# Narrow sample tables, merge ahead of residual, and a queries-and-keys stage that opens on tiles still on chip

## The reference

```python
mod = (silu(c) @ w_ada + b_ada)                       # sh1, sc1, g1, sh2, sc2, g2
h = rms_norm(x, norm1_g) * (1 + sc1) + sh1
q, k, v, u = split(h @ w_in)                          # 512, 512, 512, 1024 columns
q, k = rms_norm of each head (8 heads x 64)
new_k, new_v = the last 2048 positions of keys and values
# attention: three dilated windows (w, d) = (128, 1), (512, 4), (2048, 16): keys at distance
# 0 <= dist <= w with dist % d == 0, relative bias by log bucket, and the three outputs merged:
w = exp(m_p - max_p m_p);  o = sum(w * acc_p) / sum(w * l_p)
glu = u[:512] * sigmoid(u[512:])
dw = causal depthwise conv of glu over 31 positions (30 rows of history for the sample)
o_conv = silu(layer_norm(dw)) @ w_pw2
x = x + g1 * (concat(o_attn, o_conv) @ w_o)
h2 = rms_norm(x, norm2_g) * (1 + sc2) + sh2
x = x + g2 * (square(relu(h2 @ w_ff1)) @ w_ff2)
```

## Time and profile before

| | us |
|---|---|
| median of three runs | 3102.84 (3100.72 to 3103.69) |
| profiled execution, its own time | 3098.28 |
| its span in the profile | 3096.5 |
| TensorE busy | 2817.3 (91%) |
| VectorE, ScalarE, GpSimd busy | 1349.0, 910.5, 636.4 |
| mean granted TensorE clock | 0.951 |
| stages start at | 0, 85.0, 448.5, 689.2, 1097.7, 1241.6, 1592.3 |

### The profile page before, as it was taken

How to read it: one execution, slowest core, us unless ns; L and a number is a source line. 1 busy time by engine, 2 the same in 40 slices (tenths; PEclk the granted TensorE clock), 3 DMA queues, 4 the chain that set the end, 5 groups by cost and what they waited for, 6 DMA issues and landing times. The chain is left out here.

```text
span 3096.5 us, 40055 instructions
## 1 busy us (share of the span) xinstructions
PE 2817.3 (91%) x15078; PEld 2329.9 (75%) x15078; DVE 1349.0 (44%) x3393; ACT 910.5 (29%) x2077; POOL 636.4 (21%) x420
## 2 busy tenths in 40 slices
PE   5899979969999955788869999999997999999998
PEld 2677748847777732467648888888887999999998
DVE  3148879976777532466642111122232222222223
ACT  2333311115565521344431222211131211222211
POOL 0000000000000000244423333333332323333331
PEclk6899989979999978899989999999999999999999
DMA  7566536636553374344441213131243311111112
GB/s 245 186 205 234 196 129 225 219 102 194 174 195 116 110 272 191 104 162 139 156 148 60 91 47 101 48 102 48 85 122 133 99 48 48 48 42 48 48 48 106
DMA packets 289237, 392.95 MB, mean 127 GB/s; under 512 B 30042, under 2 KB 238282, under 8 KB 282634
## 3 DMA queue, kind: packets, MB, share of 16 engines
q1 hardware_dynamic: 266194, 298.27, 29.7%
q0 software_dynamic: 5376, 81.84, 7.4%
q10 hardware_dynamic: 17476, 10.28, 1.1%
HBM read 311.63 MB, written 150.84 MB: 149 GB/s over the span
## 5 line engine op out<-in xcount | busy, mean ns | idle before, releaser
L2337 PE MATMUL ff_u_ps<-ff_h_hi,ff_w_hi 128*128 128x352 f32 (+1 forms) x1280 | 452.1, 353 | 18.8 <-DVE ff_h_lo L2255 17.2
L2338 PE MATMUL ff_u_ps<-ff_h_lo,ff_w_hi 128*128 128x352 f32 (+1 forms) x1280 | 450.0, 352 | 0.0
L2339 PE MATMUL ff_u_ps<-ff_h_hi,ff_w_lo 128*128 128x352 f32 (+1 forms) x1280 | 449.4, 351 | 0.0
L2337 PE MATMUL ff_u_ps<-ff_a_hi,ff_w_hi 128*128 128x352 f32 (+1 forms) x1280 | 449.2, 351 | 0.0
L2338 PE MATMUL ff_u_ps<-ff_a_lo,ff_w_hi 128*128 128x352 f32 (+1 forms) x1280 | 448.7, 351 | 0.0
L2339 PE MATMUL ff_u_ps<-ff_a_hi,ff_w_lo 128*128 128x352 f32 (+1 forms) x1280 | 448.2, 350 | 0.0
L2185 POOL TENSOR_TENSOR ff_w_lo<-ff_w_raw,ff_w_hi 128x1024 fp32r<-128x1024 f32 x128 | 306.6, 2395 | 570.3 <-ACT ff_w_hi L2210 570.3
L2295 DVE TENSOR_TENSOR ff_sqr<-ff_relu 128x352 f32<-128x352 f32 (+1 forms) x160 | 98.7, 617 | 640.6 <-ACT ff_relu L2238 640.6
L2278 DVE SCALAR_TENSOR_TENSOR ff_y<-ff_u_ps,modT,ff_y 128x512 f32<-128x512 f32 (+2 forms) x280 | 178.8, 644 | 432.3 <-PE ff_u_ps L2339 432.3
L2210 ACT ACTIVATE ff_w_hi<-ff_w_raw 128x1024 fp32r<-128x1024 f32 x128 | 134.7, 1052 | 626.9 <-PE ff_u_ps L2339 605.3
L2337 PEld LDWEIGHTS ff_u_ps<-ff_h_hi,ff_w_hi 128*128 128x128 f32 x1280 | 241.6, 189 | 45.0 <-POOL ff_w_lo L2185 17.3
(11 more groups left out here) (269 smaller groups left out, 4375.3 us busy)
## 6 DMA issues: line engine op xcount, KB each, us to landing
ff_w_raw<-in_w_ff_dram SPq DMA_DIRECT2D x128, 512.0 KB, 3.8
out_new_k_sample_dram<-in_cache_k_dram POOLq DMA_DIRECT2D x8, 4088.0 KB, 15.4
out_new_v_sample_dram<-in_cache_v_dram POOLq DMA_DIRECT2D x8, 4088.0 KB, 15.9
dwq<-in_w_ada_dram SPq DMA_DIRECT2D x32, 512.0 KB, 7.9
gluT<-in_cache_k_dram SPq DMA_DIRECT2D x16, 1024.0 KB, 15.0
sa_vn<-in_cache_v_dram SPq DMA_DIRECT2D x16, 1024.0 KB, 16.5
mx_acc<-acc_d SPq DMA_DIRECT2D x16, 768.0 KB, 8.2
vu_x_in<-in_x_prompt_dram SPq DMA_DIRECT2D x16, 512.0 KB, 13.5
```

What stands on the lines that cost most here:

```text
L2337: pe.matmul(out, w_hi[:, b, w], hi, start=first, stop=False)
L2338: pe.matmul(out, w_hi[:, b, w], lo, start=False, stop=False)
L2339: return pe.matmul(out, w_lo[:, b, w], hi, start=False, stop=last)
```

## The change

The diff has these parts:

- **Tables.** A pattern's table has only the columns that it can use: 4 × 128 + 4 = 516 in place of 1028. In patterns 0 and 1 these are the last 512 cached keys and the new ones, in pattern 2 the new ones and the 512 strided keys. Seven pieces (3 for the prompt, 4 of 387 columns for the sample) in place of 12, all inside the loop over k.
- **rsqrt.** A Newton step has three instructions in place of four.
- **Values stage.** The early conv operations lie on tiles 4 to 15; `store_piece(1)` and the four weight loads are issued at tile 15; the last two tiles' `h_hi`, `h_lo` stay on chip (`last_hi`, `last_lo`) and are not stored.
- **Queries and keys.** The order of tiles is 16, 15, 0, 1, ... 14 (`tile_at`). The product of z with the norm moves from VectorE to ScalarE, 16 copies with a scale (`scaled`); the key gain moves behind the late conv operations, which lie on 15 tiles.
- **Sample attention.** Queries have a semaphore of their own (`q_in`), the cached keys 8 to 15 are loaded ahead of the second half's values, softmax and values of half 0 come ahead of the transposes of half 1 on all engines, no copy of the scores, the division by the sum is part of `gather`, one of the copies of the transposed probabilities is ScalarE's, and the store of the output is waited for only in the next stage.
- **Merge stage.** Its statistics, first two accumulators and first two conv tiles are loaded in sample attention; the fold's copies come ahead of most of the splits; GpSimd merges tile i + 2 ahead of the residual of tile i; behind the loads of tile 10 two weights and four pieces of h for the MLP are loaded.
- **MLP.** It begins with these.

```diff
-SKEYS = 4 * P + 4 * P + DS
+SKEYS = 4 * P + DS
...
             for _ in range(3):
-                step(v.tensor_tensor(t, y, y, ALU.mult))
+                step(v.scalar_tensor_tensor(out=t, in0=y, scalar=-0.5, in1=y, op0=ALU.mult, op1=ALU.mult))
                 step(v.tensor_tensor(t, t, a, ALU.mult))
-                step(v.tensor_scalar(t, t, -0.5, 1.5, ALU.mult, ALU.add))
-                step(v.tensor_tensor(y, y, t, ALU.mult))
+                step(v.scalar_tensor_tensor(out=y, in0=t, scalar=1.5, in1=y, op0=ALU.add, op1=ALU.mult))
...
-                        for g in range(KT, NTB):
-                            table(g)
+                            if k < NTB:
+                                table(k)
...
+                            if i >= NT - 1:
+                                return
...
+                                sp.wait_ge(q_pe, 2 * NQ)
+                                for k in range(4):
+                                    load_qk_w(sp, k)
+                                store_piece(1)
...
-                            mine = early_ops[5 * (i - 4):5 * (i - 3) if i < NT else 2 * TAPS] if i >= 4 else []
+                            mine = early_ops[2 * TAPS * (i - 4) // 12:2 * TAPS * (i - 3) // 12] if 4 <= i < NT else []
...
+                tile_at = [NT, NT - 1] + list(range(NT - 1))
...
                         load_h(2)
-                        for i in range(NT + 1):
-                            if i + HB <= NT:
-                                load_h(i + HB)
-                            if i >= 1:
-                                store_k(i - 1)
-                            if i >= 3:
-                                store_t(i - 3)
+                        for k in range(4, KT):
+                            sp.wait_ge(w_lod, k - 3)
+                            load_qk_w(sp, k)
+                        for half in range(2):
+                            sp.dma_start(qgain[half * DH:(half + 1) * DH, :], I["q_norm_g"][0].rearrange("(d o) -> d o", o=1)).then_inc(gain_in, 16)
+                        sp.dma_start(kgain[:], I["k_norm_g"].to_broadcast([P, DH])).then_inc(gain_in, 16)
+                        for u in range(NT + 1):
+                            if u + HB <= NT:
+                                load_h(u + HB)
+                            if u >= 1:
+                                store_k(u - 1)
+                            if u >= 3:
+                                store_t(u - 3)
...
+                        def scaled(u):
+                            n = rows_of(tile_at[u])
+                            act.wait_ge(rs_done, u + 1)
+                            if u >= 2:
+                                act.wait_ge(t_pe, 2 * (u - 1))
+                                act.wait_ge(k_out[u % 2], k_stored(u - 2))
+                            for h in range(2 * H):
+                                z = z_ps[(2 * u + h // H) % 6][0:n, h % H * DH:(h % H + 1) * DH]
+                                ins = act.activation(nrm[0:n, u % 2, h * DH:(h + 1) * DH], z, ACT.Copy, scale=rsq[0:n, u % 2, h:h + 1])
+                            ins.then_inc(z_free, 1)
...
+                        squares(0)
+                        for u in range(NT + 1):
+                            scaled(u)
+                            if u + 1 <= NT:
+                                squares(u + 1)
+                            if u >= 1:
+                                turned(u - 1)
...
+                            head_norms(u)
+                            for o in range(QK_OPS * u // (NT - 1), QK_OPS * min(u + 1, NT - 1) // (NT - 1)):
                                 late_op(v, cstep, o)
+                            key_gain(u)
...
+                    sp.dma_start(vnew[:], O["new_v_sample"][0, :, WINC - DS:WINC].rearrange("b t h d -> t b (h d)")).then_inc(b_in, 16)
+                    for j in range(G):
+                        load_v(0, j, 1)
+                    for n in range(2 * G, 4 * G):
+                        load_k(n)
+                    sp.wait_ge(o_pe, 1)
                     for a in range(2):
-                        sp.dma_start(vn[:, 0, a], cache_rows(I["cache_v"], 0, a)).then_inc(v_in, 16)
-                    sp.dma_start(vnew[:], O["new_v_sample"][0, :, WINC - DS:WINC].rearrange("b t h d -> t b (h d)")).then_inc(small_in, 16)
-                    sp.dma_start(sbias[:].rearrange("p a c -> p (a c)"), sbias_d).then_inc(small_in, 16)
-                    for g in range(DB // G):
-                        for b in range(G * g, G * g + G):
-                            if b % G == 0 and g >= 1:
-                                sp.wait_ge(o_pe, g)
-                            for a in range(2):
-                                if b >= 1:
-                                    sp.dma_start(vn[:, b % G, a], cache_rows(I["cache_v"], b, a)).then_inc(v_in, 16)
-                            for n in (range(2 * b + 4, 2 * b + 6 + (b == G - 1)) if b < G else range(2 * b + 5, 2 * b + 7)):
-                                if n < 2 * DB:
-                                    load_k(n)
-                    sp.wait_ge(k_pe, 8 * DB)
-                    sp.dma_start(wp_raw, I["w_pw2"][0].rearrange("(k p) c -> p k c", p=P)).then_inc(wp_in, 16)
-                    sp.dma_start(wl_raw, I["w_o"][0, AW:D, :].rearrange("(k p) c -> p k c", p=P)).then_inc(wl_in, 16)
-                    for g in range(DB // G):
+                        for j in range(G):
+                            load_v(1, j, a)
...
+                    store_o(0)
+                    sp.wait_ge(k_pe, 8 * DB)
+                    sp.dma_start(mx_dwt[:, 0], dw_d[:, :, 0:P]).then_inc(dw_in[0], 16)
+                    sp.dma_start(wp_raw, I["w_pw2"][0].rearrange("(k p) c -> p k c", p=P)).then_inc(wp_in, 16)
+                    for a in range(3):
+                        sp.dma_start(mx_stat[:, :, a].rearrange("p i s h -> p i (s h)"),
+                                     st_d[a].rearrange("(i p) c -> p i c", p=P)).then_inc(stat_in, 16)
+                    sp.dma_start(wl_raw, I["w_o"][0, AW:D, :].rearrange("(k p) c -> p k c", p=P)).then_inc(wl_in, 16)
+                    for i in range(2):
+                        sp.dma_start(mx_acc[:, i], acc_d[:, i * P:(i + 1) * P].rearrange("a t c -> t a c")).then_inc(acc_in[i], 16)
+                    sp.dma_start(mx_dwt[:, 1], dw_d[:, :, P:2 * P]).then_inc(dw_in[1], 16)
+                    store_o(1)
...
+                        for p in range(3):
+                            ins = v.tensor_tensor_reduce(prob[:, p], s_ps[:, S_OF[p]], sbias[:, p], 1.0, -NEG, ALU.add, ALU.min, mins[:, p:p + 1])
+                        step(ins)
                         v.sem_inc(s_read, 1)
+                        step(v.tensor_reduce(mins[:, 3:4], mins[:, 0:3], AX.X, ALU.min))
+                        v.sem_inc(s_min, 1)
+                        v.wait_ge(s_exp, 3 * g + 2)
+                        step(v.tensor_tensor(prob[:, 0], prob[:, 0], prob[:, 1], ALU.add))
+                        v.wait_ge(s_exp, 3 * g + 3)
+                        v.tensor_tensor(prob[:, 0, 4 * P:SKEYS], prob[:, 0, 4 * P:SKEYS], prob[:, 2, 0:DS], ALU.add).then_inc(soft, 1)
+                        step(v.tensor_reduce(mins[:, 7:8], mins[:, 4:7], AX.X, ALU.add))
+                        step(v.reciprocal(mins[:, 7:8], mins[:, 7:8]))
...
+                    for g in range(DB // G):
+                        for n in range(2 * G * g, 2 * G * (g + 1)):
+                            for c in (0, 2):
+                                k_copy(4 * n + c)
+                        soften(g)
+                        p_copy(g)
+                        gather(g)
...
+                        if i == 10:
+                            sp.wait_ge(S["wf_pe"], NF)
+                            for f in range(2):
+                                ff_load_up(sp, f, f)
+                            for par in range(2):
+                                sp.wait_ge(h2_out[par], 16 * 2)
+                            for k in range(4):
+                                sp.dma_start(ff_h[:, k, 0:512], h2_d[:, k, 0:512]).then_inc(ff_h_in[k], 16)
...
-                        residual(i)
                         if i + 2 <= NT:
                             merge(i + 2)
+                        residual(i)
...
                     split_w(0)
-                    split_w(1)
-                    swish(0)
+                    fold_hi(0)
                     act.wait_ge(S["fac_e"], 1)
                     act.activation(fac[:], fac[:], ACT.Exp).then_inc(S["fac_x"], 1)
-                    for g in range(NF):
-                        m, cols = fold(g)
-                        act.wait_ge(S["wf_pe"], g + 1)
-                        act.activation(wo_hi[:, WU + m, cols], fold_ps[g % 3][:], ACT.Copy).then_inc(S["wf_hi"], 1)
-                        if g in (1, 3):
-                            split_w(2 + g // 2)
-                    split_mix(0)
+                    fold_hi(1)
+                    swish(0)
```

(29 more changed lines are left out.)

461 lines of the change are left out of this document (214 added, 247 removed).

## The result

The changed kernel takes 2987.92 us (median of 4 runs, 2984.96 to 2990.33), the kernel before 3101.78 on the same chips: a ratio of 0.9633, 95% interval 0.9616 to 0.9649. The forecast was 2992 with a range of 2965 to 3030. The profiled execution has a span of 2985.3 and took 2987.06, for the 2987.4 that the sum gave it; the 4.56 that the forecast added for the median came to 0.9. The only run left out as slow is one of the sixth experiment's four, 3838 us at a granted clock of 0.673.

The account below looks back on a forecast made before the run. Seven barrier-separated stages bound the kernel, gains counting only where they shorten a stage's end. Terms of 14.7, 5.3, 4.5, 8.0, 38.4, 34.6 and 5.4 sum to 110.9; 3098.28 less that, plus 4.56, gives 2992, range 2965 to 3030.

Parts of the forecast that it names:

- Stage 0: Tables stage: ends with the last weight split, fewer table copies, smaller one-hot load, three rsqrt operations off the chain; −14.7.
- Sample attention: Sample attention stage: waits for block queries, keys and softmax shortened by reordered loads and smaller tables; −38.4 (32 to 44).
- (D): Rival: sample attention gives only 24, keys 8 to 11 waiting behind first softmax and values; +14, 3006; chance 0.13.
- L = 7.1, period 16.0: Merge loop: period is 8.9 + L, L being the accumulator load's issue to landing; 13 periods 208.7, −12.8.
- (A): Whole kernel as summed: 2992, its own range 2975 to 3010; chance 0.55.
- (B): Rival, merge loop: accumulator lands no earlier than the h store did, L = 9.3, period 18.2; 3020; chance 0.15.
- (C): Rival, merge loop: shorter burst of transfers, L = 6.0, period 14.9, −14; 2978; chance 0.12.
- (E): Rival, merge loop: accumulator load lands as slowly as sample attention's value loads, 16.5; period 25.4; 3114; chance 0.05.
- MLP opening: −5.4: MLP start: two weights and four h pieces on chip save the first landing and part of a round; 4 to 6.
- Queries and keys, opening: Start of queries and keys: fewer h loads ahead of weights 4 to 7, so earlier last split; −4.5 (3 to 5.5).
- tail: End of queries and keys: no late conv operation behind the last tile but one; −8.0, ending at +19.3 (17 to 22).
- Its TensorE work is unchanged: Values stage: TensorE's work stays the same, and the −5.3 (4 to 6.6) comes from the stage's end.

Follow-up runs that it names:

- sixth experiment: Changed kernel with an unused tile of 32 bytes a partition ahead of the values stage's weights: 3000.43 us for 2987.9.
- eighth experiment: Kernel before, with a semaphore of their own for sample attention's queries, new keys and mask: 3100.62 us, run once.
- fifth: Kernel before, with an unused tile of 32 bytes a partition ahead of the values stage's h_hi: 3096.64 us for 3101.35.
- tenth: Changed kernel with accumulator and conv tile issued ahead of the x load, plus an unused 32-byte tile ahead of m_hi: 2945.12 us; without that tile 2944.35.
- second experiment: Kernel before, with only the new order on GpSimd, merge ahead of residual: 3089.89 us, ratio 0.9964.

## Why the prediction was right, point by point

**Right as mechanism and size.** Stage 0: the end is the last split, 71.6 for 70.3; in further profiles of kernels with the same stage 0 it ends between 69.0 and 75.7, and before between 85.0 and 91.8, so the 14.7 holds as a mean (14.6); its three terms were not run apart. Sample attention: the first half was done at +51.1 (52.7 forecast), the last scores at +83 (84.3), the stage at +105.1 (105.5). One step of this schedule was not as argued: the first eight key tiles did not go at the DMA's pace, TensorE waits for no key load in the stage but 8.8 us in all for the copies from PSUM. Of (D) nothing is seen either. The last three residuals: 34.7 (33.9). Preloads at tile 10: one period longer by 5.9 (5.5). The first residual of the merge stage ended at +51.7 (54.0), a little better, but how the opening's parts divide was not run.

**Right mechanism, wrong size.** "L = 7.1, period 16.0": the term was the h store's part of the burst, taken at its bytes, 1.2. The row shows L at 7.8, the loop's median is 7.6, and the twelve undisturbed periods are 16.5: with the h store out of the burst the accumulator lands 0.5 to 0.6 sooner, not 1.2. The thirteen periods are 220.9 for the 214.2 of the sum, preloads included, 6.7 more; the earlier first residual gives 2.3 of it back, which leaves the stage's 4.9. The formula 8.9 + L holds: 16.5 with the median. The period lies between (A) and (B), nearer to (A): what was argued, 1.2, was less than half right. (C) falls, and (E) too. The Trainium skill ("DMA: Bandwidth & Descriptors", Anatomy of one DMA) gives its fit for a single DMA issued from GpSimd. Used in the prediction for SyncE's burst, it made an estimate of 5.9 behind the accumulator's issue; the trace has 7.8, so the row was the better guide.

"MLP opening: −5.4": it gave 1.8. Of the chain that ended last in the kernel after, the opening:

```profile
1484.53 2.43 DVE ff_h_lo L2315
...
1486.98 4.67 DMA gluT<-h_d
...
1494.37 3.54 DMA gluT<-h_d
...
1499.97 3.46 DMA gluT<-h_d
...
1505.10 2.37 POOL ff_w_lo L2245
```

Four pieces of h are on chip, but the load of the fifth needs a slot that the first one's split must free, so three rounds of load and split follow all the same, and TensorE runs without a gap from +24.6 for 26.3. The step that failed is "saves the first landing and part of a round": the first landing was saved, 4.1, but nothing of a round, and 2.3 went back, since the three rounds' landings take 4.67, 3.54 and 3.46 where they took 3.81, 2.77 and 2.79. Why they are longer, no run shows.

"Queries and keys, opening" and "tail": 6.7 and 9.1 against 4.5 and 8.0; why each gave more was not run. The 16 scaled copies took 3.38 us, 0.21 each, for the 0.25 taken; TensorE did not wait for them in the loop, and the steady part is as forecast.

```profile
622.65 3.38 ACT L1038 ACTIVATE qk_nrm<-qk_z_ps,qk_rsq 128x64 f32<-128x64 f32 x16 [2.78 <-DVEq L1067]
```

The prediction's estimate of 240 ns each, from the Trainium skill ("ScalarE: Activation LUTs", What ACT_TABLE_LOAD costs), is above this row.

**Wrong.** "Its TensorE work is unchanged" of the values stage. The instructions are the same 1748, but TensorE's busy time fell from 343.3 to 335.4, and the stage's products end 7.5 earlier. The fifth and sixth experiments show the cause: the edit that keeps activations on chip also moved the tiles in memory. The end of the stage gave 4.2 of the 5.3. A forecast that reads only instructions and waits can't see this term; it was 7% of the gain, and of the size of several that were argued at length.

Also wrong is a sentence of the list in sample attention, that the stage waited for the block queries behind the bias table. The idle time of 15.44 is real, and the eighth experiment shows that nobody waited for it. The sum did not use it.

**Still open.** How the 26 us of sample attention divide, and what besides equal remainders the fast spacing asks for.

## What to carry to other kernels

When two pieces of work change places on an in-order engine, look at which wait the second now stands behind, and at the queue that issues what it waits for: here the new order opened one ring and closed another, and taking the load's issue from behind a wait that it didn't need was then worth more (43.6 us) than the order itself (7.7). An idle engine in a profile is a gain only if somebody waits for it; ask who, before it enters a list. If a change moves tiles in on-chip memory, compare the spacing of unchanged matmuls first.

## What the runs showed of the hardware

- The spacing of 512-column f32r products, with a clock of 1.00 granted throughout, was 227.3 ns or 233.3 ns depending on where the operands' tiles start: fast when both have the same remainder by 64 bytes. An unused tile of 32 bytes a partition switched it either way (fifth and sixth), but moved it by only 1.5 ns in the merge stage (tenth).
- Stage 0, whose last splits wait 2.3 to 2.7 us each for their weights' loads, differed by up to 7 us between executions of the same instructions (69.0 to 75.7). The runs of the changed kernel spread over 5 us; whether stage 0 makes that spread was not looked at.
- A 768 KB load landed after 7.8 us (median of thirteen 7.6) with 1.3 MB of other transfers in flight, and after 8.3 (8.2) with another 512 KB.
- A VectorE operation on 32x1024 took 3.77 us beside a GpSimd product on 128x1536 and 1.20 without it, and the product 3.75 for 2.76 (second experiment).
